# Two trunk layers on one core: the context tile's layer-0 expert pass is computed inside the RWKV scan

## The reference

```python
def peer(h, w_q, keys, u_tab, v_tab):           # per block of 128 tokens xb
    q = (xb @ w_q).reshape(BLOCK, PEER_HEADS, D_QUERY)
    s1 = einsum('thd,hnd->thn', q[..., :half], keys[0])
    s2 = einsum('thd,hnd->thn', q[..., half:], keys[1])
    v1, i1 = top_k(s1, 16); v2, i2 = top_k(s2, 16)
    cand = v1[..., :, None] + v2[..., None, :]
    sv, pos = top_k(cand.reshape(BLOCK, 8, 256), 16)
    eidx = ...                                  # expert number of each pick
    act = gelu(einsum('thkd,td->thk', u_tab[eidx], xb))
    return einsum('thk,thkd->td', softmax(sv) * act, v_tab[eidx])

def step(s, inp):                               # the scan, 8 heads, two directions
    s = s * w - (s @ kh)[..., None] * ka + v[..., None] * kt
    return s, s @ r
```

## Time and profile before

| what | us |
|---|---|
| median of 3 runs (4475.11 to 4486.43) | 4482.62 |
| the profiled execution | 4476.27 |
| its span in the trace | 4474.5 |
| mean granted TensorE clock | 0.872 |
| busy: TensorE / VectorE / ScalarE / GpSimd | 3168 / 2767 / 1713 / 1459 |
| read from device memory | 1531 MB |

### The profile page before, as it was taken

One profiled execution on the slowest core, in us unless ns is written; L12 is line 12 of the kernel. 1 busy time (PEld: TensorE's weight loads), 2 busy tenths in 40 slices (PEclk: granted clock), 3 DMA queues, 4 the chain that ended last, 5 costly groups with the idle time before them and its releaser, 6 DMA issues.

```text
span 4474.5 us, 71248 instructions
## 1 busy us (share of the span) xinstructions
PE 3168.1 (71%) x26559; PEld 1569.7 (35%) x26559; DVE 2767.3 (62%) x7107; ACT 1713.2 (38%) x5328; POOL 1459.1 (33%) x1298
## 2 busy tenths in 40 slices
PE   7978788868865557776667766786786687666555
PEld 4534577343321114431323432352452153132111
DVE  1256644266647766776657776766676776665764
ACT  1036322033323334543324563554463363332332
POOL 0000000023334444443433443444344434434443
PEclk9997799889987778987889998898998898888777
DMA  5162000189999999999999999999999999999998
GB/s 223 52 239 87 15 7 9 54 323 397 404 374 421 421 415 417 420 408 419 418 420 408 420 418 412 414 419 403 411 419 420 411 419 416 416 416 420 413 419 338
DMA packets 238219, 1538.81 MB, mean 344 GB/s; under 512 B 33223, under 2 KB 34338, under 8 KB 67506
## 3 DMA queue, kind: packets, MB, share of 16 engines
q0 software_dynamic: 184768, 1342.45, 72.8%
q1 hardware_dynamic: 52664, 191.69, 11.1%
q10 hardware_dynamic: 442, 0.12, 0.0%
HBM read 1531.06 MB, written 3.10 MB: 343 GB/s over the span
## 4 chain that ended last, share of the span: by engine, by line
DMA 43%; PE 16%; DVE 8%; ACT 6%; issue 4%; POOL 4%; SPq 0%; POOLq 0%; ACTq 0%; PEldq 0%; DVEq 0%
DMA t_ring<-in_peer_uv,t_eidx 40%; PE t_ps L2217 10%; DVE t_ring L1691 5%; POOL t_ring L1565 4%; ACT t_dg L1857 2%; PE t_ps L2112 1%; PE t_ps L2042 1%; DMA t_wq<-in_cv_w_pw 1%; ACT t_wgt L1851 1%; DMA t_wg<-in_cv_w_pw 1%; ACT t_wgt L1846 1%; PE t_ps L2218 1%; PE t_ps L2153 1%; PE t_ps L2228 0%; PE t_ps L2180 0%
## 5 line engine op out<-in xcount | busy, mean ns | idle before, releaser
L1565 POOL DMA_INDIRECT t_ring<-in_peer_uv,t_eidx x1280 | 1451.6, 1134 | 2982.9 <-PE t_ps L2221 1842.6
L2217 PE MATMUL t_ps<-t_ring,t_dg 64*64 64x512 f32 x2560 | 1534.2, 730 | 1058.6 <-ACT t_dg L1857 1038.0
L1691 DVE SCALAR_TENSOR_TENSOR t_ring<-t_ring,t_hring 128x1024 f32<-128x1024 f32 x1024 | 1252.8, 1224 | 816.7 <-DMA t_ring<-in_peer_uv,t_eidx 814.3
L2221 PE MATMUL t_ps<-t_ring,t_dg 64*64 64x512 f32 x2560 | 1552.3, 737 | 0.0
L2220 PE MATMUL t_ps<-t_ring,t_dg 64*64 64x512 f32 x2560 | 1552.0, 737 | 0.0
L2218 PE MATMUL t_ps<-t_ring,t_dg 64*64 64x512 f32 x2560 | 1551.6, 737 | 0.0
L2217 PEld LDWEIGHTS t_ps<-t_ring,t_dg 64*64 64x64 f32 x2560 | 338.1, 153 | 1976.6 <-issue 1946.3
L1846 ACT ACTIVATE t_wgt<-t_dots 128x2 f32<-128x2 f32 x640 | 130.2, 203 | 1943.4 <-DVE t_ring L1691 1942.4
L1691 DVE SCALAR_TENSOR_TENSOR t_ring<-t_ring,t_early 128x1024 f32<-128x1024 f32 x256 | 314.0, 1226 | 260.0 <-DMA t_ring<-in_peer_uv,t_eidx 260.0
L1857 ACT ACTIVATE t_dg<-t_eye,t_wgt 128x64 f32<-128x64 f32 x1280 | 376.3, 340 | 1.8 <-ACT t_wgt L1851 1.1
L2221 PEld LDWEIGHTS t_ps<-t_ring,t_dg 64*64 64x64 f32 x2560 | 339.2, 153 | 0.0
(11 more groups left out here) (362 smaller groups left out, 4436.2 us busy)
## 6 DMA issues: line engine op xcount, KB each, us to landing
t_wq<-in_peer_w_q SPq DMA_DIRECT2D x112, 512.0 KB, 8.1
ev_mod_ring<-in_mod_w SPq DMA_DIRECT2D x48, 1024.0 KB, 10.1
t_wg<-in_cv_w_pw SPq DMA_DIRECT2D x48, 512.0 KB, 8.0
t_ring<-in_peer_uv,t_eidx POOLq DMA_INDIRECT x1280, 12.8
t_wq<-in_cv_w_pw SPq DMA_DIRECT2D x40, 512.0 KB, 8.3
ev_wring<-in_ab_w_in SPq DMA_DIRECT2D x21, 512.0 KB, 3.6
ev_qk<-in_ab_w_out SPq DMA_DIRECT2D x1, 4096.0 KB, 12.0
t_lrow<-modrows SPq DMA_DIRECT2D x6, 512.0 KB, 16.9
```

The lines of the kernel that those rows point to most:

```text
L1565: pool.indirect_dma_start(ring[:, place[n], :], None, table, bass.IndirectOffsetOnAxis(ap=eidx[:, s % 2, r:r + 1], axis=0)).then_inc(row_i ...
L1691: V.scalar_tensor_tensor(ring[:, place[n], 0:D], ring[:, place[n], 0:D], 1.0, h_of(j), ALU.mult, ALU.mult, accum_out=dots[:, j % 2, r:r + ...
L2217: nc.tensor.matmul(straight[low, cols], dg[low, n % DIAGS, :], ring[low, one, rows], **ends)
L2221: second = nc.tensor.matmul(crossed[low, cols], dg[high, (n + 1) % DIAGS, :], ring[high, two, rows], **ends)
```

## The change

Pass 0 (the context tile's layer-0 experts) leaves the trunk and is done in `phase_scan`, beside the eight chunks of the latents. What it needs there comes with it for tile 0: the scan's output norm, the output projection with its weights loaded in eight pieces through two buffers, the residual, norm, modulation, turning, the 16 blocks of queries and scores, the choices and 128 gathers. A chunk counts 24 ticks (4 for each of five levels and 4 for the end), and every engine calls its generators after each tick's own step:

```diff
+    PLACES, DIAGS, NC = 6, 6, 2 * PH
+    TICKS = 24
+    C = TICKS * N_P
+    chunk_tick = lambda i, k: TICKS * i + k
+    query_tick = lambda b: C + 18 + b if b < 4 else C + 22 + 7 * (b - 4)
+    dot_tick = lambda r: C + 33 + 6 * r // 5
+    weigh_tick = lambda c: dot_tick(2 * c + 1) + 2
+    sum_tick = lambda c: dot_tick(2 * c + 1) + 4
+    exp_tick = lambda hd: C + 30 if hd == 0 else C + 30 + 13 * hd
...
+    LAST = chunk_tick(N, 0)
...
+    ring = [buf[:, 2048 * a:2048 * (a + 1)] for buf in (rows4, spilled_mix, done_qk) for a in range(2)]
...
+                for k in range(KD):
+                    if k >= 2:
+                        sp.wait_ge(cj["wo_used"], k - 1)
+                    sp.dma_start(wide_w[k % 2], io["ab_w_out"][:, k * D:(k + 1) * D]).then_inc(wo_in[k % 2], 16)
...
+                    else:
+                        sp.wait_ge(S["wq_used"], b - 1)
+                        sp.wait_ge(S["s_done"], b - 1)
+                    sp.dma_start(wide_w[b % 2], io["peer_w_q"][0, b]).then_inc(E.wq_in[b % 2], 16)
...
+                for r in range(PICKS):
+                    if r % TOPK == 0:
+                        pool.wait_ge(S["chosen"], r // TOPK + 1)
+                    if r >= PLACES:
+                        pool.wait_ge(S["used"], r - PLACES + 1)
+                    elif r == 2:
+                        pool.wait_ge(cj["spilled"], 16)
```

**PSUM.** The experts take four banks, so the scan keeps two for each direction. Preparation and inversion now share banks, and waits are added:

```diff
-    region = lambda g, r: ps[:, g, r // 2, r % 2]
+    region = lambda g, r: ps[:, 2 * g + r // 4, r % 2]
...
                 def refine(g, i, l):
                     pe.wait_ge(m_set[g], LEVELS * i + l + 1)
...
+                            pe.wait_ge(y_set[g], i)
+                        else:
+                            pe.wait_ge(bd_set[g], 1)
+                    elif i + 1 < N:
+                        prelude_read = (None, (kT_set, 2), (va_set, 2), (ae_set, 2), (bd_set, 1))[l]
+                        pe.wait_ge(prelude_read[0][g], prelude_read[1] * (i + 2))
...
                 def weigh_state(g, i):
...
+                    pe.wait_ge(x_set[g], LEVELS * i + 1)
...
-                        act.wait_ge(s_done[g], i + 1)
-                        nc.scalar.copy(q2[:, g, :, cols(g, i)], region(g, 5)).then_inc(y_set[g], 1)
+                        act.wait_ge(s_set[g], 2 * i + 1)
+                        nc.scalar.copy(operand(Q2, g, i), region(g, 5)).then_inc(y_set[g], 1)
```

**After the scan.** `phase_scan_out` and `phase_outproj` work on the latents' 512 tokens alone. The trunk starts at pass 1, which uses six places as pass 0 did; five of the latents' 16 score blocks come before its first pick and the others beside it:

```diff
-    place = [n % (R - 2) if n < PICKS else (R - 2 + n - PICKS) % R for n in range(JOBS * PICKS)]
+    place = [n % (R - 2) if n < 2 * PICKS else (R - 2 + n - 2 * PICKS) % R for n in range(JOBS * PICKS)]
...
-    score_tick = lambda b: 26 + 2 * (11 * b // 4)
+    score_tick = lambda b: -1 if b < 5 else 2 + 6 * (b - 5)
...
-                for s in range(JOBS):
+                for s in range(1, JOBS):
```

More of the change, by code:

```diff
@@ new lines, in gate_head, with __init__, run @@
+def gate_head(dve, V, S, own, after_own, w, j, hd):
+    part = w.gate[:, j % 2, hd * TOPK:(hd + 1) * TOPK]
+    for _ in range(3):
+        yield
+    dve.wait_ge(S["exp_ready"], j * PH + hd + 1)
+    own(V.tensor_reduce(w.esum[:], part, AXX, ALU.add))
+    yield
+    after_own()
+    own(V.reciprocal(w.rsum[:], w.esum[:]))
+    yield
+    after_own()
+    V.tensor_scalar(part, part, w.rsum[:, 0:1], None, ALU.mult).then_inc(S["gate_ready"], 1)
+    yield
+class Side:
+    def __init__(self, steps):
+        self.steps, self.at = steps, next(steps, None)
+    def run(self, tick):
+        while self.at is not None and self.at <= tick:
+            self.at = next(self.steps, None)
@@ new lines, in run_sides, with __init__ @@
+def run_sides(sides, tick):
+    for side in sides:
+        side.run(tick)
+class Choice:
+    def __init__(self, **buffers):
+        self.cands, self.iota, self.top, self.topi, self.best, self.besti = (buffers[n] for n in ("cands", "iota", "top", "topi", "best", "besti"))
+        self.part, self.half, self.eidf, self.eidx, self.gate, self.esum, self.rsum = (
+            buffers[n] for n in ("part", "half", "eidf", "eidx", "gate", "esum", "rsum"))
+        self.sub = self.cands[:, 1, :].rearrange("p (a n) -> p a n", a=2)
@@ new lines, with __init__ @@
+class Expert:
+    def __init__(self, K):
+        self.S = {n: K.sem("t_" + n) for n in (
+            "squares", "mean", "root", "rstd", "scaled", "h_done", "turned", "hT_done", "iota_in", "keys_in",
+            "q_done", "q_copied", "s_done", "s_copied", "wq_used", "grow_in", "own", "chosen", "over_done", "exp_ready",
+            "gate_ready", "eye_in", "u_used", "gelu_done", "wgt_done", "diag_set", "used", "crossed_out", "joined", "gated", "summed")}
+        self.wq_in = [K.sem(f"t_wq_in{a}") for a in range(2)]
+        self.count = [0]
@@ new lines, in phase_scan @@
+        ss, ms, rt, rstd = (norm[:, n:n + 1] for n in range(4))
+        singles = job("singles", (P, 2))
+        choice = Choice(cands=cands, iota=iota, top=job("top", (P, 2, TOPK)), topi=job("topi", (P, 2, TOPK), U32),
+                        best=spare[:, 384:512].rearrange("p (h n) -> p h n", h=PH), besti=job("besti", (P, TOPK), U32),
+                        part=job("part", (P, 2, TOPK), U32), half=job("half", (P, 2, TOPK)), eidf=job("eidf", (P, TOPK)),
+                        eidx=u[:, 0, 8:9, :].bitcast(U32), gate=u[:, 0, 10:11, :], esum=singles[:, 0:1], rsum=singles[:, 1:2])
@@ new lines, in choices @@
+                def choices():
+                    tick, left = C + 22, iter(())
+                    for hd in range(PH):
+                        steps = choose_head(dve, Vx, S, own, after_own, choice, 0, hd, [cscores[:, hd % 4, a, :] for a in range(2)], 2 * (hd + 1))
+                        for n in range(13):
+                            yield tick
+                            if hd == 0 and n == 0:
+                                dve.wait_ge(S["iota_in"], 16)
+                            next(steps, None)
+                            next(left, None)
+                            tick += n % 2 if hd == 0 else 1
+                        left = gate_head(dve, Vx, S, own, after_own, choice, 0, hd)
+                    for _ in range(7):
+                        yield tick
+                        next(left, None)
+                        tick += 1
@@ L1288, in _ @@
             def _(sp):
-                for s in range(2):
-                    load_row(sp, K, rows[:, s, :], s, 0, 2, rows_in)
+                load_row(sp, K, row[:], 1, 0, 2, row_in)
             @block.tensor
@@ L1591, in modulate_all @@
                 def modulate_all():
-                    mean(0)
-                    for t in range(NT):
+                    mean(1)
+                    for t in range(1, NT):
                         if t + 1 < NT:
@@ L1825, in _ @@
                         dot(s, r)
-                        for _ in range(2 if s == 0 and r < G else 1):
-                            next(beside, None)
+                        next(beside, None)
                     assert next(beside, None) is None
```

827 lines of the change are left out of this document (514 added, 313 removed).

## The result

The changed kernel takes 4507.3 us in the median of seven runs, the kernel before 4478.2 beside it: a ratio of 1.0057 (95% interval 1.0037 to 1.0076), slower by 29 us. Forecast were 4391. Its profiled execution took 4510.5 us, with a span of 4508.6. Over both measurements its runs spread from 4494 to 4529 us, those of before beside them from 4465 to 4489; a single profile of it is good to some 10 us.

A forecast was written before the change was run, and what follows sets the result against it. The prediction took the scan as TensorE-bound (82% busy) and the expert passes as DMA-bound (0.99 to 1.00). Its terms, -339 - 15 + 2 + 260 = -92 us, gave 4384, on the median 4391; range 4340 to 4510.

The forecast's parts named there:

- Part 1: Trunk's start to pass 2: pass 0 gone, pass 1 opens the trunk; 401 us in place of 740, a gain of 339.
- Part 2: Between scan and trunk: one of five output-projection tiles goes, 4 MB come back from memory; -15 us (-18 to -10).
- Part 3 (a): Scan in four PSUM banks: refinements held back until a bank is read; 3 us a chunk, +6 on the context's two chunks.
- (b): Scan, positions 0 to 33: context output, scores and first choice take 98 us, today 38.5; ends 80 and 110.
- (c): Scan's 128 gathers: 2.85 us each, 366 us, nearer to DMA's floor than to the far end; ends 340 and 460.
- DMA's floor: Scan's gathers: 128 x 2.6 = 333 us, with 12 query loads about 349, the highest of the floors.
- Rival 2: Scan's gathers: six ring places set the pace, dots wait for landings; 3.3 us a gather, 422 us, 4447; chance 0.18.
- Rival 1: Scan: VectorE's and TensorE's added work lie one behind the other; 546 us in place of 366, 4571; chance 0.22.
- Rival 3: Scan's gathers: TensorE's clock falls to 0.75, its 298 us become 397; 445 us, kernel 4470; chance 0.05.
- Rival 4: Scan: the change hides everything, gathers at the floor, 345 us, context output and first choice 85; kernel 4357; chance 0.10.
- The rule against it: Scan's gathers: VectorE dots with two SBUF inputs lock out GpSimd's issues; 2.85 + 0.6 us a gather, +77 us.
- the mark: Sign for the forecast in the gathers' stretch of the scan: DMA share 0.85 or more.

The follow-up runs named there:

- few_picks: Changed kernel with 8 of the scan's 128 gathers, dots, weighings and sums; chunks 39.0, 40.2, 34.9 us with choices, 27.5 and 28.0 without.
- rows_later: Changed kernel with only the scaling of hmean and its wait for the rows moved from before the scan to its second chunk; 4514.3 us, 1.0089.
- plus3_alone: Changed kernel with only weighings 1 and sums 3 positions behind the pair's second dot, instead of 2 and 4; 4465.2 us, 0.9976.
- small_rows: Changed kernel with the scan's gathers cut to 256 of 2048 columns, dots' products set to zero; chunks 70.5, 70.1, 63.0 us with choices, 55.9, 55.7 without.
- all_small: Changed kernel with gathers an eighth of a row, dots over 128 columns, sums over 64; chunks 55.4, 55.7, 41.6 us with choices, 37.8, 37.2 without.
- short_sums_small_rows: Changed kernel with sums over 64 of 512 columns and gathers an eighth of a row, dots whole; chunks 58.3, 68.2, 56.7 us with choices, 52.3, 48.4 without.

## Why the prediction was wrong, step by step

**Part 1, the trunk loses a pass: -309 instead of -339.** The first gather came 57 us after the start (forecast 55). The first freed place came at 86, where 70 was taken and 87 named as the bad end, for another reason than the one given: not the clock, but gates spread over six picks, since the change had taken out the doubled steps of the choices. That is 16 of the 30 us missed. The step that failed is reading the opening of pass 0 as that of pass 1 without going through what `next(beside)` does in it. The other 14: the 122 picks behind took 345 us, not 331. The prediction took the 13 loads fewer off at an unchanged 396 GB/s; they ran at 383, at a DMA share of 0.98, where the same picks of pass 0 had 397 at 1.00. Why is not shown.

**Part 2: -13.3 instead of -15.** Right.

**Part 3 (a), four banks: 0 instead of +3 a chunk.** The bound from the rows was sound (0 to 5); the value was taken too high. few_picks shows 27.5 and 28.0. The 31.7 us of the context's second chunk are something else: a copy of W lies some 10 us behind its chunk's start, so that span takes in the first positions of the context's output.

**(b), positions 0 to 33: about 103 us instead of 98.** From 571.6 (the third copy of W at 581.6, less those 10 us) to the first gather at 674.2. Right. few_picks has the same first chunk of the latents (89.9 us against 91.1), so these are projection, norm and queries, as priced.

**The start, +8, was in no term.** VectorE's side work begins with a wait for the rows of gains, and it is run when it is made, before the masks. By rows_later 5 us of it are that wait.

**(c), the gathers: 434 us between first and last issue, 445 to the last dot, instead of 366.** This is the term that turned the sign; it alone is 79 us of the scan's 91. DMA's floor was right: 20 gathers at 2.6 us are 52, and with a seventh place the last two chunks take 54.7. Wrong was "nearer to the floor", taken from pass 0 with the same six places. There a place had its next gather 5.9 us after the pair's second dot began; here it is 9.6, since the sum stands four positions behind by the schedule's own `sum_tick`. The prediction's numbers would have shown it: at 366 us for 152 positions one is 2.4 us long, so the two to three left for a gather are 5 to 7 us, and a landing takes 5.6 at the least and 12.8 in the median, plus the issue. Rival 2 says it, but with positions of 1.6 to 2.2 us and a chance of 0.18. The step that failed is this overlap, landings taken as covered by six places. Released one position earlier, the gathers come 3.12 us apart instead of 3.42 (669.1 to 1065.8 in plus3_alone), 38 us of the 72 that they ran over the forecast's 362; with the seventh place it is 3.06. The last two chunks are then at 58 and 55 us, the forecast's 57. What is left lies mostly in the chunks with choices, 66 us with the earlier release, and there small_rows and few_picks point to the engines' work in a row, which the prediction took as hidden under DMA's floor.

**The rivals.** Rival 2 (places) is shown: five places cost 84 us, an earlier sum gives 41, a seventh place some 8 more. Rival 1 (work in a row) is shown too, at 28 us a chunk for 20 picks instead of its 45, in the chunks without choices and with small rows; 10 of the 28 are weighing and hand-overs, which no term had. Beside the choices it is the larger part, since small rows leave 67.9 of 70.3 us. The two were priced as alternatives. They are one loop: shortening one leg (dots, sums) alone changed nothing, moving the sum too far forward moved the wait from VectorE to TensorE. Rival 3 falls at its price: the granted clock was 0.89 in the stretch, not 0.75, and TensorE was busy 314 us, not 397. But 0.89 is below the scan's 0.99 and just below the 0.9 named, TensorE's 298 us were 16 short, and what the clock costs was not measured by itself. Rival 4 falls.

**The rule against it.** Its sum, 2.85 + 0.6 = 3.45 us a gather, is the measured 3.42, and it is a coincidence. GpSimd's issue took 1058 to 1122 ns in the mean in the three buffers and, with dots of an eighth the width, 943 to 948, while the gathers came no faster. Dots hold an issue back by about 0.15 us in the mean, not by 0.6, and GpSimd is busy 140 of 435 us. In the changed kernel 75 of the 128 issues overlap a dot, and they take 1207 ns in the mean, the other 53 take 946. The direction is that of the Trainium skill (SBUF — State Buffer, Who interferes with whom); the price took a whole dot of 1.2 us as held back in each pair, where an issue that meets a dot loses 0.26 us in the mean.

**What was to be seen.** Pass 2's first gather came 527 us after the scan's end (forecast 495). DMA at 0.85 met the mark that I had set for the forecast and still belonged to a pace of 3.42 us: it moved 316 GB/s, where pass 0 moved 396 at 0.99, so the mark was too weak. VectorE's waits on landings were named as the sign of rival 2, rightly.

## What to carry to other kernels

When a ring of buffers is served inside another schedule, count the round of one place in positions (landing, use, release) and multiply by the length that a position will have once the work is in it, not by today's. What is left between release and next use must exceed a landing; if it doesn't, release earlier by a position at a time and watch which engine's wait grows. Here floors of 80% and more on engines that hand over to each other did not stand beside each other: the chain took up part of each pick's work, and a third of what it took up was weighing and hand-overs. Before comparing two schedules by single traces, see whether their unexplained gaps are alike.

## What the runs showed of the hardware

A pick with an eighth of the row, a narrow dot and short sums still lengthens the chunk by 0.49 us, weighing on ScalarE and hand-overs between the engines together (all_small, few_picks). An issue of a gather on GpSimd that overlaps a VectorE dot over 1024 columns takes 1207 ns in the mean, one that doesn't 946. With the same matmuls to do, TensorE was busy 27.3 us a chunk at a granted clock of 0.97 (all_small) and 36.5 at 0.79 (short_sums_small_rows). The same scan code summed to 561.3 and 559.7 us over nine chunks in two traces with 14 and 12 unexplained gaps of TensorE, and to 574.9 in one with 60.
